# Query products of the routing made from rounded and remainder parts

## The reference

```python
def _peer(h, wq, subkeys, U, V):
    hf = h.reshape(T, D)                                    # T = 512, D = 1024
    q = (hf @ wq).reshape(T, PEER_HEADS, 2, PEER_HALF)      # 8 heads, 2 halves of 128
    s = jnp.einsum('thcd,hcnd->thcn', q, subkeys)           # 128 subkeys per half
    sv, si = lax.top_k(s, PEER_TOPK)                        # 16 of 128
    cand = sv[:, :, 0, :, None] + sv[:, :, 1, None, :]
    ...
    fv, fpos = lax.top_k(cand..., PEER_TOPK)                # 16 of 256 pairs
    gates = jax.nn.softmax(fv, axis=-1)
    # y = sum over the picked experts of gate * gelu(u . h) * v
```

## Time and profile before

| | |
|---|---|
| median of three runs | 2102.45 us (2098.7 to 2104.54) |
| profiled execution | 2104.01 us, its span 2102.3 us |
| TensorE busy | 1918.7 us, 91% |
| VectorE busy | 1428.1 us, 68% |
| ScalarE busy | 734.1 us, 35% |
| GpSimd busy | 550.0 us, 26% |
| query products (L1641) | 256 records, 114.3 us busy |

### The profile page before, as it was taken

How to read it: one execution, slowest core, us unless ns; L and a number is a source line. 1 busy time by engine, 2 the same in 40 slices (tenths; PEclk the granted TensorE clock), 3 DMA queues, 4 the chain that set the end, 5 groups by cost and what they waited for, 6 DMA issues and landing times.

```text
span 2102.3 us, 33108 instructions
## 1 busy us (share of the span) xinstructions
PE 1918.7 (91%) x10322; PEld 1602.1 (76%) x10322; DVE 1428.1 (68%) x2902; ACT 734.1 (35%) x1305; POOL 550.0 (26%) x427
## 2 busy tenths in 40 slices
PE   2889896786967999999999999999989999999996
PEld 2343585685834687879999999999988888888885
DVE  4187435445244468687488888886758888888887
ACT  1221134343222343435444444443233333333331
POOL 3011332131100222223432233224513323233310
PEclk9999998998989999999999999999999999999998
DMA  7273100000051232434589889889979999999982
GB/s 262 98 233 127 41 1 1 0 0 0 0 201 42 90 126 96 132 99 133 206 294 299 298 296 301 296 301 336 389 281 414 368 347 359 355 353 348 355 316 79
DMA packets 244203, 434.82 MB, mean 207 GB/s; under 512 B 84578, under 2 KB 157636, under 8 KB 244164
## 3 DMA queue, kind: packets, MB, share of 16 engines
q1 hardware_dynamic: 207300, 300.12, 41.2%
q0 software_dynamic: 36864, 134.23, 17.5%
HBM read 379.77 MB, written 54.53 MB: 207 GB/s over the span
## 4 chain that ended last, share of the span: by engine, by line
PE 65%; DVE 1%; DMA 1%; issue 1%; ACT 0%; SPq 0%; ACTq 0%; DVEq 0%
PE bank L1315 25%; PE bank L1706 8%; PE bank L1704 8%; PE bank L1705 8%; PE bank L1641 5%; PE bank L1295 5%; PE bank L1687 4%; DMA urows<-in_peer_u 1%; PE bank L1653 1%; DVE n_stats L1118 0%; DVE wide L2008 0%; DVE wide L2006 0%; DVE wide L1127 0%; SPq L1539 0%; SPq L1543 0%
## 5 line engine op out<-in xcount | busy, mean ns | idle before, releaser
L1315 PE MATMUL bank<-hh,uh 128*128 128x384 f32 x1024 | 358.3, 350 | 0.0
L1315 PE MATMUL bank<-hl,uh 128*128 128x384 f32 x1024 | 344.4, 336 | 0.0
L1704 PE MATMUL bank<-vh,wh 128*128 128x512 f32 x768 | 299.4, 390 | 3.1 <-DVE wl L1967 3.1
L1706 PE MATMUL bank<-vh,wl 128*128 128x512 f32 x768 | 299.5, 390 | 0.0
L1705 PE MATMUL bank<-vl,wh 128*128 128x512 f32 x768 | 299.4, 390 | 0.0
L1373 POOL DMA_INDIRECT vsel<-in_peer_v,picks x128 | 151.7, 1185 | 413.0 <-DVE gt L1399 398.7
L1800 ACT ACTIVATE vh<-vraw 128x1024 fp32r<-128x1024 f32 x128 | 135.9, 1062 | 288.4 <-PE bank L1706 270.2
L1373 POOL DMA_INDIRECT usel<-in_peer_u,picks x108 | 147.9, 1369 | 247.9 <-DVE usel L1380 234.6
L1964 DVE TENSOR_TENSOR vl<-vraw,vh 128x1024 fp32r<-128x1024 f32 x128 | 156.6, 1223 | 81.1 <-ACT vh L1800 81.0
L1315 PE MATMUL bank<-hh,ul 128*128 128x384 f32 x1024 | 198.3, 334 | 0.0
L1315 PEld LDWEIGHTS bank<-hl,uh 128*128 128x128 f32 x1024 | 194.4, 190 | 0.0
(11 more groups left out here) (314 smaller groups left out, 3096.3 us busy)
## 6 DMA issues: line engine op xcount, KB each, us to landing
urows<-in_peer_u SPq DMA_DIRECT2D x128, 512.0 KB
vraw<-in_peer_v SPq DMA_DIRECT2D x128, 512.0 KB
ada<-in_ada_w SPq DMA_DIRECT2D x12, 2048.0 KB
scored<-act_out SPq DMA_DIRECT2D x128, 192.0 KB
gates<-SS SPq DMA_DIRECT2D x16, 1536.0 KB
gtile<-gates SPq DMA_DIRECT2D x32, 768.0 KB
act_in<-scored SPq DMA_DIRECT2D x128, 192.0 KB
wt<-in_w_in SPq DMA_DIRECT2D x19, 512.0 KB
```

What stands on the lines that cost most here:

```text
L1315: last = pe.matmul(bank, u[:, k, :], h[:, k, :], start=(n == 0), stop=(n == 3 * KD - 1))
L1704: pe.matmul(b, wh[s][:, cols], vh[s][:, half], start=first, stop=False)
L1706: last = pe.matmul(b, wl[s][:, cols], vh[s][:, half], start=False, stop=stop)
```

## The change

The query product of the routing is made like the expert products: the weights `wq[c]` are rounded to `wqh[c]` by ScalarE, the remainder `wql[c]` is made by GpSimd, and TensorE makes 24 rounded matmuls (`wqh` with `hh`, `wqh` with `hl`, `wql` with `hh`) of 512 columns instead of eight plain ones. `hh` and `hl` become 512 tokens wide, so `emit_mix_out` also splits the last tile. ScalarE and GpSimd make the first head's parts ahead of the loop, and each next head's inside the turn before: ScalarE ahead of the evacuations of steps 2 and 3, GpSimd behind the remainders of steps 1 and 2. SyncE waits for `wql` instead of the product before it loads `wq[c]` anew. To make room, three of the tiles for picked rows move into `h2`, and `OI` and `OJ` move from `h2` to parts of `SS`, `st2` and `q2`.

```diff
-        hh = keep("hh", [P, KD, TD], F32R)
-        hl = keep("hl", [P, KD, TD], F32R)
+        hh = keep("hh", [P, KD, T], F32R)
+        hl = keep("hl", [P, KD, T], F32R)
...
-        usel = [keep(f"usel{k}", [P, D]) for k in range(3)] + [uraw[:, :, :].rearrange("p k e -> p (k e)")]
+        h2 = wide
+        halves = [h2[:, 2 * k:2 * k + 2, :].rearrange("p k t -> p (k t)") for k in range(3)]
+        usel = halves + [uraw[:, :, :].rearrange("p k e -> p (k e)")]
...
                 if t >= 1:
                     split(dve, t - 1)
+            split(dve, NT - 1)
...
-            last = pe.matmul(bank, u[:, k, :], h[:, k, :], start=(n == 0), stop=(n == 3 * KD - 1))
+            last = pe.matmul(bank, u[:, k, :], h[:, k, 0:TD], start=(n == 0), stop=(n == 3 * KD - 1))
...
+        wqh, wql = ([rt(f"{n}{c}", [P, KD, P], F32R) for c in range(2)] for n in ("wqh", "wql"))
...
-        OI, OJ = ([h2[:, SLOTS * j + q, :].rearrange("p (t n) -> p t n", t=4) for q in range(SLOTS)]
-                  for j in range(2))
+        OI = [SS[:, 3, 0:4, :], SS[:, 3, 4:8, :], st2[:, 4:8, :]]
+        OJ = [SS[:, 7, 0:4, :], SS[:, 7, 4:8, :], q2[0][:, :].rearrange("p (t n) -> p t n", t=4)]
...
                 for c in range(2):
-                    sp.wait_ge(q_up, START + 2 * i + (c + 1))
+                    sp.wait_ge(wql_up[c], START + i + 1)
                     sp.dma_start(wq[c][:, :, :], wv[:, :, bass.ds((2 * nxt + c) * P, P)]).then_inc(wq_in[c], 16)
...
-            with pool.Fori(0, SPREAD) as i:
+            def query_rest(i, c):
+
+                pool.wait_ge(wqh_up[c], START + i + 1)
+                pool.wait_ge(q_up, START + 2 * i + (c - 1))
+                pool.tensor_tensor(wql[c][:, :, :], wq[c][:, :, :], wqh[c][:, :, :].bitcast(F32), ALU.subtract)\
+                    .then_inc(wql_up[c], 1)
+            for c in range(2):
+                query_rest(0, c)
+            with pool.Fori(0, ROUTED - 1) as i:
+                for s in range(4):
+                    scores.remainder(pool, i, s)
+                    if s in (1, 2):
+                        query_rest(i + 1, s - 1)
+            with pool.Fori(ROUTED - 1, SPREAD) as i:
                 for s in range(4):
                     scores.remainder(pool, i, s)
...
                 for c in range(2):
-                    pe.wait_ge(wq_in[c], START + 16 * i)
+                    pe.wait_ge(wqh_up[c], START + i + 1)
                     pe.wait_ge(q_out, START + 2 * i)
-                    for k in range(KD):
-                        last = pe.matmul(banks[4 + c][:, :], wq[c][:, k, :], h2[:, k, :], start=(k == 0),
-                                         stop=(k == KD - 1))
+                    steps = [(wqh[c], hh, k) for k in range(KD)] + [(wqh[c], hl, k) for k in range(KD)]
+                    steps += [(wql[c], hh, k) for k in range(KD)]
+                    for n, (m, h, k) in enumerate(steps):
+                        if n == 2 * KD:
+                            pe.wait_ge(wql_up[c], START + i + 1)
+                        last = pe.matmul(banks[4 + c][:, :], m[:, k, :], h[:, k, :], start=(n == 0),
+                                         stop=(n == 3 * KD - 1))
...
+            def query_round(i, c):
+                act.wait_ge(wq_in[c], START + 16 * i)
+                act.wait_ge(q_up, START + 2 * i + (c - 1))
+                act.activation(wqh[c][:, :, :], wq[c][:, :, :], ACT.Copy).then_inc(wqh_up[c], 1)
+            for c in range(2):
+                query_round(0, c)
...
                 for s in range(1, 4):
+                    if s < 3:
+                        query_round(i + 1, s - 1)
                     following(i, s, False)
                     scores.gelu(act, i, s)
```

More of the change, by code:

```diff
@@ L166, in hybrid_layer @@
         dots, gel, wsel = (keep(n, [P, 4]) for n in ("dots", "gel", "wsel"))
-        h2 = wide
         asked = ExitStack()
@@ L1478, in emit_experts @@
         sk_in = [sem(f"sk_in{c}") for c in range(2)]
+        wqh_up, wql_up = ([sem(f"{n}{c}") for c in range(2)] for n in ("wqh_up", "wql_up"))
         q_up, q_out, k_up, k_out, s_up, s_out = (sem(n) for n in ("q_up", "q_out", "k_up", "k_out", "s_up", "s_out"))
```

## The result

The kernel after takes 2084.93 us (2083.62 to 2086.49, four runs), the kernel before 2103.49 with one more run beside it. The ratio is 0.992, with a 95% interval of 0.9908 to 0.9933: faster by 0.8%. The forecast was 2083.4. The profiled execution took 2084.41, its span is 2082.7, so 19.6 less than the span before. The forecast sum was 19.1.

The account below looks back on a forecast made before the run. TensorE was taken to bound the routing loop. Gain 22.8 less losses 0.7, 1.0 and 2.0 made 19.1 us, taking the median 2102.45 to 2083.4, range 2076.5 to 2092.

Parts of the forecast that it names:

- The bound: Routing loop: TensorE alone sets the pace, busy 36.00 of 36.00 us, so time taken off it comes off the end.
- The query products: Routing loop: 24 rounded matmuls at 0.227 us take 5.44 instead of 6.87, gaining 1.43 for each of 16, 22.8 us.
- the estimate of 2079.2: Query products at the Trainium skill's 216 ns a matmul: 5.18 us each, gain 27.0 us, time 2079.2.
- The change of kind: Second query product, behind the subkeys' turn: one added change from plain to rounded matmuls per iteration, 8 x 0.09 = 0.7 us lost.
- ScalarE and GpSimd in the loop: Routing loop: two copies of 1.06 us and two subtractions of 2.40 an iteration stay hidden; tightest margin 1.0 us.
- The first rival: Routing loop: ScalarE or GpSimd comes late past the 1.0 us margin, time between 2083.4 and 2097.6; chance 0.12.
- GpSimd against VectorE: Routing loop: the new GpSimd work misses VectorE's two-input operations, except expert 3's remainder for half a microsecond; VectorE doesn't become the bound.
- Ahead of the loop: Before the routing loop: ScalarE's first rounding copy loses 1.0 us; the last tile's split in the stage before loses 2.0.
- The first product: First query product, 9.24 us, partly at the lower clock in both kernels: the same gain of 1.43 taken.
- the second rival: Barrier hides the split, the clock rises earlier in the first product, or matmuls beat 0.227: 2079 to 2081; chance 0.10.
- The moved tiles: One-hot operands and picked rows in new places keep shape, type and order: cost 0.
- time moving in the stages behind: Stages behind the routing loop, held to be unchanged: time moving there would show the prediction wrong.

Follow-up runs that it names:

- the first two experiments: Kernel after with query-product matmuls reordered so 8 of 24 repeat the stationary tile: 2085.63 us; kernel after with expert products' first 16 matmuls in two runs of eight: 2085.79.
- the block walk: Kernel after with half 0's stationary tile always block 0 and half 1's moving tile always block 0: query product 5.62 us in both halves.
- one other place: Kernel after with the tiles of rounded weights and remainders allotted first, some 50 KB lower in each partition: 2086.13 us, query product 5.62.
- the doubled kernel: Kernel after with each of GpSimd's two remainder subtractions of an iteration made twice: 2124.45 us, ratio to before 1.0108.
- the second profile: Kernel after, unchanged, run and profiled again on one chip with the kernel before: 2083.98 us, ratio 0.992.

## Why the prediction held, step by step

**The bound.** Right: TensorE was busy for 33.00 of 33.00 us in the loop, and what left it left the end. The fifth row of the table is 15 x 1.25 = 18.75 to 0.02.

**The query products.** Right in mechanism, the term too large: 1.25 for each and not 1.43, 20.0 us and not 22.8. The step that failed is the pace of 0.227 taken from the weighted sum; here it is 0.234. The prediction called that "this very shape" with "a new stationary tile for each", which isn't so for one matmul in three. That difference isn't the cause, as the first two experiments show; nor is the block walk, nor the place as far as one other place tells. So the cause of this miss stays open. The period came to 33.46 where 33.2 was forecast.

The Trainium skill (TensorE: Matmul & The Clock Gate, "Back-to-back issue gap") has its 216 ns for isolated matmuls and a shorter 131 ns for a sustained stream. The measured 234 ns agrees with neither, and the trace decides against the estimate of 2079.2.

**The change of kind.** Wrong, 0 instead of 0.7: the product behind the subkeys' turn takes 5.62 like the one behind a rounded product, and the period fell by 2 x 1.25 exactly. What the earlier trace rows shows at the start of an expert product is the same in both kernels.

**ScalarE and GpSimd in the loop.** Right: nothing is late, shown by the period of 35.96 in the kernel that makes the parts and doesn't use them. Timeline of POOL, kernel after:

```profile
740.70 2.40 POOL L1607 TENSOR_TENSOR wql<-wq,wqh 128x1024 fp32r<-128x1024 f32 x1 [4.24 <-ACT wqh L1773]
743.07 2.40 POOL L1340 TENSOR_TENSOR ul<-uraw,uh 128x1024 fp32r<-128x1024 f32 x1
745.43 2.40 POOL L1607 TENSOR_TENSOR wql<-wq,wqh 128x1024 fp32r<-128x1024 f32 x1
747.78 2.40 POOL L1340 TENSOR_TENSOR ul<-uraw,uh 128x1024 fp32r<-128x1024 f32 x1
```

The remainder of expert 2 ends at 745.47; its product begins at 744.02 in the chain and wants it 2.8 later, less the 0.2 between chain and timeline: about 1.1 of margin, forecast 1.0. What I left out is a wait on ScalarE: its raw copy waits for GpSimd 14 times, 9.4 us in all, and is still in time. The first rival's point of decision was placed rightly, as the doubled kernel shows with its first wait of 1.17. Its price counted the waits alone; the doubled kernel lost 14.8 us more than it waited, at a lower granted clock.

**GpSimd against VectorE.** In the doubled kernel a GpSimd operation that began at 758.85 took 3.39 us, where 2.40 is usual, with a two-input operation of VectorE from 758.78 to 759.99 beside it. That is the other side of what the earlier trace rows showed, where VectorE was the one held up. The exclusive lock of the Trainium skill (SBUF — State Buffer, "Who interferes with whom") agrees with both. In the kernel after, the two new operations take 2.39 to 2.42 in all 16 cases: they meet nobody, as worked out.

**Ahead of the loop.** The split cost 2.15 for 2.0, and the barrier is released by VectorE's end, as I took it, 3.6 us ahead of the next stage. The first copy cost 0.72 for 1.0. Both are right in kind and near in size.

**The first product.** It gave 3.36 instead of 1.43. That was the second rival's early clock, which the profiled execution met by 2.1 us beyond the 1.25. In the second profile of the same kernel the gain was 1.83 (9.24 to 7.41).

**The moved tiles.** Wrong: 0 was forecast, and it was about 2 us. From the exponential to the end the two profiles with the old places took 1084.4 and 1084.2, the twelve with the new ones 1084.8 to 1087.3, 1086.4 in the middle. "Cost 0" had rested on shape, type and order being kept; where a tile lies wasn't weighed. The prediction named time moving in the stages behind as a sign of being wrong, and in this term it was.

**The sum as measured**: 20.0 - 2.15 - 0.72 - 2.07 = 15.1, and 2.1 for the clock in the first product 17.2. With the first product of the second profile it is 15.7. The medians say 18.6 and 18.2, or 16.5 against the ten runs of the kernel before built once more. What is left is within the scatter of the runs, and of the stages ahead, 2.45 in the profiled pair. So the nearness of the forecast's 19.1 is luck: a term too large by 2.8 and a cost not seen, 2.0, stood against a gain of the clock that it hadn't counted, 2.1, a loss that wasn't there, 0.7, and 2.45 of scatter in the profiled pair.

## What to carry to other kernels

Where one engine is busy without a gap, its saved time comes off the end and can be summed from the chain, but the pace of the new form should carry a margin of some per cent even when the same shape stands elsewhere in the trace. Work given to engines beside it is free only up to a margin that can be worked out from the timeline, wait by wait. Past it the waits are not the whole price: in the doubled kernel the granted clock fell behind them, and 23.6 us of waiting came with 14.8 us of slower work. So where TensorE begins to wait, read its granted clock too. A moved tile is a part of the change and wants a price, and a gain of a few microseconds should be read from the pieces of the profile, since first rows like these move by as much.

## What the runs showed of the hardware

- 24 rounded matmuls of 512 columns took 5.62 us in the query product, 5.49 with other stationary tiles, and 0.227 each in the weighted sum; of 384 columns 4.17 in both places. The cause isn't known.
- The stationary tile of the matmul before, used again, saved nothing: a query product took 5.62 with and without it, an expert product 4.17, and each matmul still had its own weight load of 0.19 us.
- The clock granted to TensorE rose and fell again within one product of 7.41 us in a profile of a kernel whose other profile had 5.88.
- In the doubled kernel TensorE stood still for 2.75 us (up to 764.60), the granted clock was 0.50 from 766 to 769, and a query product took 6.96 us instead of 5.62.
- A GpSimd subtraction of 128x1024 took 3.39 us instead of 2.40 when a two-input operation of VectorE had begun 0.07 us before it.
- From VectorE's last operation to the first of the next stage, over a barrier of all engines, it was 3.60 and 3.61 us.
- With the one-hot operands and picked rows in other places, half a turn of an otherwise equal loop took 12.80 us instead of 12.75.
